# Projections by seven block products, three edits to attention, rows and last sums, in a 256-token layer stack of fp32

## Chip, cores and metric

The kernel runs on one core of a Trainium2 chip. The metric is the device time of one execution in microseconds; the kernel before has a median of 1836.27 us over 3 runs. TensorE multiplies matrices; VectorE (DVE), ScalarE (ACT) and GpSimd (POOL) do the element-wise work; SyncE (SP) issues the loads of weights. Each engine runs its own program, in order, and they meet at semaphores.

## What is computed

256 tokens of width 1024 in fp32 pass one hybrid layer (two kinds of attention, then a mixture of 16384 single-neuron experts) and then a second block of two layers (mixer, cross attention, convolutional feed-forward), which the change does not touch. The hybrid layer, cut:

```python
def hybrid_layer(x, cos, sin, norm1_g, w_in, ..., w_out, norm2_g, peer_wq, peer_k1, peer_k2, peer_u, peer_v):
    h = rmsnorm(x, norm1_g)
    (aq, ak, av, bq, bkc, bvc, bks, bvs, bkw, bvw, bgate, mgate) = split_columns(h @ w_in)
    ...
    ya = moba_attention(qa, ka, heads(av, A_HEADS)).reshape(B, S, A_WIDTH)
    ...
    yb = nsa_attention(qb, kc, vc, ks, heads(bvs, B_KV_HEADS), kw, heads(bvw, B_KV_HEADS), gb)
    ...
    merged = g[:, :, 0] * (ya @ w_up_a) + g[:, :, 1] * (yb @ w_up_b)
    x = x + merged @ w_out
    return x + peer_ffn(rmsnorm(x, norm2_g), peer_wq, peer_k1, peer_k2, peer_u, peer_v)

def peer_ffn(h, w_q, sub_k1, sub_k2, expert_u, expert_v):
    ...
    def per_chunk(args):
        xc, ec, gc = args
        u = expert_u[ec]
        a = jnp.einsum('cd,chkd->chk', xc, u).astype(jnp.float32)
        w = (jax.nn.gelu(a) * gc).astype(xc.dtype)
        return jnp.einsum('chk,chkd->cd', w, expert_v[ec])
```

In the experts each token has 8 heads; a head takes the best 16 of 128 by each half key and then the best 16 of their 256 pairs. The first 2560 of the columns of `h @ w_in` (queries, keys, values of both attentions) are the projections that the change rewrites.

## The kernel before

**Weights.** They come as slots of 1 MB into a ring of 4 slots, issued by SP in the fixed order of the program: key and value weights of the cross attention, projections (`proj`, 10 slots, two for each 512 columns), compression, gates, merge, output, routing queries, and 128 + 128 slots of experts. A slot is loaded again once TensorE is through with the one four places earlier (`slot_done`).

**Projections.** VectorE normalises x (`rms_rows`, L1490 to 1509) and TensorE turns it to `xT`. Meanwhile TensorE does memory keys (`feature_major`, L442). Then, for each of five chunks `c` of 512 columns, TensorE does two token tiles x eight k tiles of 512 columns (L556 to 565, matmul L451); ScalarE copies the two PSUM banks to `qkv` (L1171). VectorE clears and casts some tiles (L1512 to 1517), normalises and rotates the heads in four groups (`head_norm`, L1520 to 1569), makes the shifted and position-added copies (L1578 to 1587). TensorE goes on with gates (L569, L442) and turns the heads (L590).

**Attention.** 16 units, first eight of the one kind ("moba"), then eight of the other ("nsa"), in a pipeline of hand-written order. In step u TensorE does the scores of unit u (L617 to 637), the filling work (L682 to 714), then `turn_probs(u - 1)` (L640 to 654) and `values(u - 2)` (L656 to 678). VectorE takes maxima (L1602) and scales (L1626 to 1638), ScalarE takes exponentials and copies the turned probabilities (L1213 to 1225). The scores of unit u wait for `probT_ready` of unit u - 1.

**Experts.** 152 tokens are computed densely: each block of 128 experts is a matmul against all of them (`up_block` L827, `down_block` L835), with the gates from VectorE. The other 104 "sparse" tokens get the rows of their chosen experts by indirect DMA from GpSimd (L2271), 107 of `u_rows` and 107 of `v_rows`, each for up to 128 token-expert pairs, into seven buffers (`ROWS`). VectorE takes a dot product with each u row (`row_dots`, L1749) and later adds each v row, weighted (`row_adds`, L1850). Routing on VectorE is, for the second token tile, a loop over eight heads (L1794 to 1802: best 16, candidates, `pick` L1765 to 1786 after each four), then the loop over tiles (L1805 to 1835), in which the row numbers and gates are staged for GpSimd (L1820 to 1828). Dots go in numbers fixed by constants: up to `DOTS_ROUTING` between routing steps, up to `DOTS_FIRST` before the selection `sel` that TensorE needs for its first expert block (L1859); the rest is mixed among the gate work of the blocks. `LAST_ADDS` row sums stand at the end between the residual of the first token tile (L1916) and the fold of the sparse tokens (TensorE, L954); the second block starts on the first token tile at L922.

## Time and profile before

| quantity | value |
|---|---|
| median of 3 runs | 1836.27 us (1835.15 to 1836.65) |
| profiled execution | 1835.7 us, of which 1833.9 us are the span of the trace |
| mean granted clock of TensorE | 0.984 of full speed |
| busy share of TensorE, its weight loads | 96%, 81% |
| busy share of VectorE, ScalarE, GpSimd | 56%, 14%, 16% |
| DMA | 439.57 MB, mean 240 GB/s |

The trace has one row per instruction or group of like ones, with start, length and, where the engine stood idle before, what it waited for. The views used are the page's busy shares, the list of waits of an engine (what it waited for, in sum), the chain that ended last, groups of instructions of one line and shape, the timeline of an engine, and windows (busy time of each engine in a stretch with granted clock and share of the DMA). Along the span the DMA is above 0.9 of its capacity at 415 GB/s from about 440 to 1040 us, and at a third to a half elsewhere.

### The profile page before, as it was taken

How to read it: one execution, taken by the hardware profiler on the slowest of the kernel's cores; microseconds unless marked ns; L12 is line 12 of the kernel's file. 1: busy time of each engine (PE TensorE's matmuls, PEld its weight loads, DVE VectorE, ACT ScalarE, POOL GpSimd, SP SyncE). 2: the span in 40 equal slices, each digit the busy share in tenths (PEclk: the TensorE clock that was granted, in tenths of full speed). 3: DMA queues.
4: the chain of work that ended last, by engine and by line, in shares of the span. 5: the costliest groups of instructions: out<-in, count | busy, mean ns of one | idle time of the engine just before them, and what ended most of it. 6: DMA issues, size and time to landing. Idle time of an engine off the chain costs nothing.

```text
span 1833.9 us, 28803 instructions
## 1 busy us (share of the span) xinstructions
PE 1767.6 (96%) x11513; PEld 1477.1 (81%) x11513; DVE 1032.5 (56%) x2254; ACT 254.9 (14%) x603; POOL 295.1 (16%) x280
## 2 busy tenths in 40 slices
PE   8999989999999999999999689999999999999996
PEld 6478647886999999999999566789965977699942
DVE  1421342386964988899443653259984213269964
ACT  1013540120444111000000010111100001111100
POOL 0200000003333454344332510000000000000000
PEclk9999999999999999999999789999999999999998
DMA  7435232437999999999999963274454434354551
GB/s 277 162 124 175 72 113 92 166 117 286 418 416 416 414 416 411 369 415 414 416 416 418 368 259 115 92 252 162 165 180 159 162 138 148 128 184 161 171 174 46
DMA packets 76397, 439.57 MB, mean 240 GB/s; under 512 B 8530, under 2 KB 8560, under 8 KB 37504
## 3 DMA queue, kind: packets, MB, share of 16 engines
q1 hardware_dynamic: 42336, 304.11, 44.2%
q0 software_dynamic: 32528, 126.44, 17.5%
q10 hardware_dynamic: 1424, 7.47, 1.0%
q8 instruction: 80, 1.31, 0.3%
q14 instruction: 29, 0.24, 0.0%
HBM read 432.67 MB, written 5.24 MB: 239 GB/s over the span
## 4 chain that ended last, share of the span: by engine, by line
PE 70%; DMA 13%; DVE 9%; issue 6%; ACT 1%; POOL 0%; DVEq 0%; POOLq 0%
PE ps L1067 12%; PE ps L484 10%; PE ps L526 8%; PE ps L827 7%; PE ps L835 7%; PE ps L442 6%; DMA arena<-v_rows,sparse_pairs 6%; DMA arena<-u_rows,sparse_pairs 6%; PE ps L1088 4%; PE ps L451 4%; DVE arena L1850 2%; DVE arena L1749 2%; PE ps L695 2%; PE ps L742 2%; PE ps L848 1%
## 5 line engine op out<-in xcount | busy, mean ns | idle before, releaser
L827 PE MATMUL ps<-xT,ring 128*128 128x152 f32 x2048 | 271.6, 294 | 3.5 <-DVE sel L1859 3.4
L827 PEld LDWEIGHTS ps<-xT,ring 128*128 128x128 f32 x2048 | 267.2, 191 | 4.4 <-DVE sel L1859 3.7
L835 PE MATMUL ps<-arena,ring 128*128 128x152 f32 (+1 forms) x2048 | 269.6, 293 | 0.1
L835 PEld LDWEIGHTS ps<-arena,ring 128*128 128x128 f32 x2048 | 265.5, 190 | 0.8 <-issue 0.8
L484 PE MATMUL ps<-ring,arena 128*128 128x512 f32 x416 | 181.4, 592 | 0.4 <-ACT arena L1371 0.4
L1850 DVE SCALAR_TENSOR_TENSOR arena<-arena,sparse_dots 128x1024 f32<-128x1024 f32 x105 | 134.7, 1283 | 76.1 <-DMA arena<-v_rows,sparse_pairs 68.4
L526 PEld LDWEIGHTS ps<-xT,ring 128*128 128x128 f32 x1536 | 173.4, 192 | 3.0 <-issue 2.9
L526 PE MATMUL ps<-xT,ring 128*128 128x128 f32 x1536 | 174.1, 275 | 0.0
L1749 DVE CUSTOM_DVE_ANT_0 arena<-arena 128x1024 f32<-128x1024 f32 x107 | 128.2, 1223 | 78.6 <-DMA arena<-u_rows,sparse_pairs 71.3
L2271 POOL DMA_INDIRECT arena<-u_rows,sparse_pairs x107 | 129.7, 1213 | 188.9 <-DVE sparse_dots L1749 153.5
L2271 POOL DMA_INDIRECT arena<-v_rows,sparse_pairs x107 | 130.2, 1216 | 179.8 <-DVE arena L1850 121.6
L2236 POOL TENSOR_SCALAR stat<-stat 128x1 f32<-128x1 f32 (+2 forms) x23 | 4.4, 190 | 942.5 <-DVE stat L2014 711.9
L484 PEld LDWEIGHTS ps<-ring,arena 128*128 128x128 f32 x416 | 78.0, 190 | 93.0 <-issue 92.1
L442 PE MATMUL ps<-xT,ring 128*128 128x256 f32 x544 | 121.4, 386 | 0.0
L442 PEld LDWEIGHTS ps<-xT,ring 128*128 128x128 f32 x544 | 105.1, 194 | 14.6
L1067 PE MATMUL ps<-arena 128*128 128x128 f32 x864 | 102.4, 275 | 0.0
L1067 PEld LDWEIGHTS ps<-arena 128*128 128x128 f32 x864 | 99.4, 192 | 0.0
L1067 PE MATMUL ps<-xT,ring 128*128 128x128 f32 x576 | 70.2, 275 | 0.0
L1602 DVE CUSTOM_DVE_ANT_0 arena<-ps,small 128x128 f32<-128x128 f32 (+1 forms) x48 | 14.6, 355 | 97.0 <-PE ps L630 65.6
L451 PE MATMUL ps<-ring,xT 128*128 128x512 f32 x160 | 68.8, 592 | 0.0
L1067 PEld LDWEIGHTS ps<-xT,ring 128*128 128x128 f32 x576 | 67.2, 192 | 0.0
L451 PEld LDWEIGHTS ps<-ring,xT 128*128 128x128 f32 x160 | 30.4, 190 | 37.8 <-issue 37.8
(305 smaller groups left out, 2108.0 us busy)
## 6 DMA issues: line engine op xcount, KB each, us to landing
ring<-stream SPq DMA_DIRECT2D x288, 1024.0 KB
arena<-second_params POOLq DMA_DIRECT2D x6, 1024.0 KB, 5.2
arena<-kv_scratch POOLq DMA_DIRECT2D x2, 2048.0 KB, 13.3
kv_scratch<-arena POOLq DMA_DIRECT2D x2, 1024.0 KB, 6.7
kv_scratch<-arena ACTq DMA_DIRECT2D x2, 1024.0 KB
arena<-held_params ACTq DMA_DIRECT2D x1, 2048.0 KB
arena<-u_rows,sparse_pairs POOLq DMA_INDIRECT x107
arena<-v_rows,sparse_pairs POOLq DMA_INDIRECT x107
```

What stands on the lines that cost most here:

```text
L442: ins = pe.matmul(ps[:, bank, t * T:(t + 1) * T], w[:, k * 2 * P + t * P:k * 2 * P + (t + 1) * P], act[:, k, :], start=(k == 0), stop=(k = ...
L451: ins = pe.matmul(ps[:, bank0 + i, :], act[:, k0 + k, i * P:(i + 1) * P], w[:, k * 512:(k + 1) * 512], start=(first_k and k == 0), stop=(l ...
L484: ins = pe.matmul(ps[:, bank0 + 2 * i + hf, :], act_of(2 * s + k, i), held[s][:, k * D + hf * 512:k * D + (hf + 1) * 512], start=(bank0 + ...
L526: ins = pe.matmul(ps[:, bank, t * T + i * P:t * T + (i + 1) * P], held[s][:, k * 2 * P + t * P:k * 2 * P + (t + 1) * P], xT[:, k, i * P:(i ...
L695: ins = pe.matmul(ps[:, 6, t * T:(t + 1) * T], w[:, k * 2 * P + t * P:k * 2 * P + (t + 1) * P], xT[:, k, :], start=(k == 0), stop=(k == KT ...
L827: ins = pe.matmul(ps[:, o % 2, 0:DENSE], w[:, (o % 2) * D + k * P:(o % 2) * D + (k + 1) * P], xT[:, k, 0:DENSE], start=(k == 0), stop=(k = ...
L835: ins = pe.matmul(ps[:, 4 + k // 2, c:c + DENSE], w[:, (o % 2) * D + k * P:(o % 2) * D + (k + 1) * P], H[:, n, :], start=False, stop=last, ...
L1067: ins = pe.matmul(ps[:, bank + b, c * P:(c + 1) * P], weight[:, k, :], x[:, k, :], start=(k == 0), stop=(k == 3))
L1088: return pe.matmul(ps[:, bank, :], x, weight, start=(m == 0), stop=(m == FT_PAIRS - 1 and bank < 4))
L1749: dve.tensor_tensor_reduce(fetched[:, b, :], fetched[:, b, :], x_sparse[:, m // PAIRS_HALF, :], 1.0, 0.0, ALU.mult, ALU.add, dots[:, 0, m: ...
L1850: dve.scalar_tensor_tensor(total, fetched[:, b, :], dots[:, 0, m:m + 1], total, ALU.mult, ALU.add).then_inc(row_added, 1)
L2271: pool.indirect_dma_start(fetched[:, b, :], None, table, bass.IndirectOffsetOnAxis(ap=pairs[:, 0, m:m + 1].bitcast(U32), axis=0), bounds_c ...
```

## The change

**Projections.** Each chunk of 512 columns is made as a 2 x 2 by 2 x 2 block product (token tiles x halves of k, halves of k x halves of columns) with seven block products in place of eight. VectorE makes four sums of weight blocks (`sums_of_proj`) for each chunk and four sums of blocks of `xT` once, and puts the seven products together (`add_proj`); ScalarE copies the first product only. The order on VectorE is written out anew: the clears and casts and the second to fourth head norms stand behind output sums. `qkv_copied` gives way to five semaphores.
**Attention.** `values(u - 2)` stands ahead of `turn_probs(u - 1)`; the scores wait for `probc_copied` of unit u - 2, and only where that unit is "nsa", instead of `probT_ready` of unit u - 1; ScalarE copies that tile first.
**Rows.** The row numbers are staged in halves, after heads 4 and 8 of the loop over heads, with two row dots behind each of heads 5 to 8; the gates are sent later. GpSimd fetches 15 rows from the first half before it waits for the second. `DOTS_ROUTING` is 38, `DOTS_FIRST` 56.
**Last sums.** `LAST_ADDS` is 16.

The diff, cut:

```diff
@@ -46,9 +46,12 @@
 CHUNKS = PAIRS_HALF + PAIRS_B
-DOTS_ROUTING = 30
-DOTS_FIRST = 50
-LAST_ADDS = 21
+PH_LATE = 4
+DOTS_HEAD = 2
+DOTS_EARLY = DOTS_HEAD * PH_LATE
+DOTS_ROUTING = 38
+DOTS_FIRST = 56
+LAST_ADDS = 16
@@ -220,13 +223,22 @@
...
         memT = mem_raw.rearrange("p (k t) -> p k t", k=KT)
+        p_sums = [prob_and_PT[:, 0:4096].rearrange("p (s k n) -> p s k n", s=4, k=4),
+                  gT.rearrange("p j t -> p (j t)").rearrange("p (s k n) -> p s k n", s=4, k=4)]
+        px_sums = yT.rearrange("p j t -> p (j t)").rearrange("p (s k n) -> p s k n", s=4, k=4)
+        p_first = xn[:, 0, 0:512].rearrange("p (b n) -> p b n", b=2)
+        p_sum2 = xn[:, 0, 512:768]
+        p_sum43 = xn[:, 1, 0:512].rearrange("p (s n) -> p s n", s=2)
...
@@ -555,14 +569,36 @@
             for c in range(5):
...
+                b0, sums = 4 * (1 - c % 2), p_sums[c % 2]
...
+                def product(b, half, x, weight):
+                    for k in range(4):
+                        ins = pe.matmul(ps[:, b0 + b, half * T:(half + 1) * T], x[:, k, :], weight[:, k, :],
+                                        start=(k == 0), stop=(k == 3))
+                    return ins
+                if c < 2:
+                    pe.wait_ge(xkv_ready, 1)
                 else:
...
-                for kh in range(2):
-                    w = slot("proj", 2 * c + kh)
-                    token_major(w, 4 + 2 * (c % 2), xT, 4 * kh, 4, kh == 0, kh == 1)\
-                        .then_inc(slot_done, 1)
+                    pe.wait_ge(proj_added, c - 1)
+                w1 = slot("proj", 2 * c).rearrange("p (k n) -> p k n", k=4)
+                product(0, 0, x11, w1[:, :, 0:T])
+                w2 = slot("proj", 2 * c + 1).rearrange("p (k n) -> p k n", k=4)
+                product(0, 1, x12, w2[:, :, 0:T]).then_inc(proj_psum, 1)
+                if c == 0:
+                    pe.wait_ge(xkv_ready, 3)
+                    pe.wait_ge(proj_x_ready, 1)
+                product(2, 0, x4, w2[:, :, T:2 * T])
+                pe.wait_ge(proj_w_ready, c + 1)
+                product(1, 0, x1, sums[:, 0]).then_inc(slot_done, 1)
+                product(1, 1, x3, sums[:, 2]).then_inc(slot_done, 1)
+                if c == 0:
+                    pe.wait_ge(xkv_ready, 4)
+                product(3, 0, x2, sums[:, 1])
+                product(2, 1, x22, sums[:, 3]).then_inc(proj_psum, 1)
+            pe.wait_ge(proj_added, 4)
@@ -579,7 +615,7 @@
-            pe.wait_ge(qkv_copied, 10)
+            pe.wait_ge(proj_added, 5)
@@ -622,7 +658,8 @@
                     pe.wait_ge(max_ready, u if kind == "nsa" else u - 1)
-                    pe.wait_ge(probT_ready, u - 1)
+                    if units[u - 2][0] == "nsa":
+                        pe.wait_ge(probc_copied, u - 1 - NU // 2)
@@ -725,10 +762,10 @@
                     fill(u)
+                if u >= 2:
+                    values(u - 2)
                     turn_probs(u - 1)
-                if u >= 2:
-                    values(u - 2)
@@ -1166,10 +1203,8 @@
             for c in range(5):
-                act.wait_ge(slot_done, START["proj"] + 2 * c + 2)
-                for i in range(TT):
-                    act.copy(qkv[:, i, c * 512:(c + 1) * 512], ps[:, 4 + 2 * (c % 2) + i, :])\
-                        .then_inc(qkv_copied, 1)
+                act.wait_ge(proj_psum, 2 * c + 1)
+                act.copy(p_first[:, c % 2, :], ps[:, 4 * (1 - c % 2), 0:T]).then_inc(proj_first, 1)
@@ -1217,11 +1252,11 @@
                 pt = PT[:, u % 2].rearrange("p k n -> p (k n)")
+                if kind == "nsa":
+                    act.copy(pt[:, 8 * P:9 * P], ps[:, 2 * (u % 2), 0:P]).then_inc(probc_copied, 1)
                     ins = act.copy(pt[:, a * P:a * P + w], ps[:, 4 + a // 4, 0:w])
-                if kind == "nsa":
-                    ins = act.copy(pt[:, 8 * P:9 * P], ps[:, 2 * (u % 2), 0:P])
...
@@ -1484,6 +1519,34 @@
+            def sums_of_proj(c):
+                w1, w2, w3, w4 = (p_sums[c % 2][:, n] for n in range(4))
+                wb = []
+                for n in (START["proj"] + 2 * c, START["proj"] + 2 * c + 1):
+                    dve.wait_ge(loaded[n % RING], 16 * (n // RING + 1))
+                    w = ring[:, n % RING, :].rearrange("p (k n) -> p k n", k=4)
+                    wb += [w[:, :, 0:T], w[:, :, T:2 * T]]
+                w11, w12, w21, w22 = wb
+                link(dve.tensor_tensor(w1, w12, w11, ALU.subtract))
+                dve.tensor_tensor(w3, w22, w12, ALU.subtract)
+                link(dve.tensor_tensor(w2, w22, w1, ALU.subtract))
+                dve.tensor_tensor(w4, w21, w2, ALU.subtract).then_inc(proj_w_ready, 1)
+            def add_proj(c):
+                b0, col = 4 * (1 - c % 2), 512 * c
+                dve.wait_ge(proj_first, c + 1)
+                dve.wait_ge(proj_psum, 2 * c + 2)
+                link(dve.tensor_tensor(p_sum2, p_first[:, c % 2, :], ps[:, b0 + 3, 0:T], ALU.add))
+                dve.tensor_tensor(qkv[:, 0, col:col + T], p_first[:, c % 2, :], ps[:, b0, T:2 * T], ALU.add)
+                link(dve.tensor_tensor(p_sum43, p_sum2.unsqueeze(1).to_broadcast([P, 2, T]),
+                                       ps[:, b0 + 1, :].rearrange("p (s n) -> p s n", s=2), ALU.add))
+                dve.tensor_tensor(qkv[:, 0, col + T:col + 2 * T], p_sum43[:, 0, :], ps[:, b0 + 2, 0:T], ALU.add)
+                dve.tensor_tensor(qkv[:, 1, col:col + T], p_sum43[:, 1, :], ps[:, b0 + 2, T:2 * T], ALU.add)
+                dve.tensor_tensor(qkv[:, 1, col + T:col + 2 * T], p_sum43[:, 1, :], ps[:, b0 + 1, 0:T], ALU.add)\
+                    .then_inc(proj_added, 1)
...
@@ -1509,20 +1573,22 @@
             rms_rows(0)
...
+            dve.wait_ge(xT_by_dve, 4)
...
+            link(dve.tensor_tensor(x2, x1, x11, ALU.subtract))
+            dve.tensor_tensor(x3, x11, x21, ALU.subtract)
+            dve.tensor_tensor(x4, x12, x2, ALU.subtract).then_inc(proj_x_ready, 1)
+            sums_of_proj(1)
                 chunk = c0 // 512
-                dve.wait_ge(qkv_copied, 2 * chunk + 2)
+                dve.wait_ge(proj_added, chunk + 1)
@@ -1568,8 +1634,24 @@
-            for grp in range(4):
-                head_norm(grp)
+            add_proj(0)
+            sums_of_proj(2)
+            head_norm(0)
+            add_proj(1)
+            sums_of_proj(3)
...
+            add_proj(2)
+            sums_of_proj(4)
+            add_proj(3)
+            add_proj(4)
+            head_norm(1)
+            head_norm(2)
+            head_norm(3)
@@ -1789,6 +1871,19 @@
+            def stage_rows(half):
...
+                first, second = (routed[rows, 1, n, half * PAIRS_HALF:(half + 1) * PAIRS_HALF]
+                                 .rearrange("p (m r) -> p r m", r=2) for n in range(2))
+                for r, dst in enumerate((pairs, pairs_out)):
+                    ins = dve.scalar_tensor_tensor(dst[rows, 0, c].bitcast(U32), first[:, r], float(P), second[:, r],
+                                                   ALU.mult, ALU.add)
+                ins.then_inc(pairs_staged, 1)
+                if half == 0:
+                    dve.wait_ge(x_sparse_ready, 1)
@@ -1798,10 +1893,12 @@
                     shift_gates()
+                if h >= PH - PH_LATE:
+                    row_dots(DOTS_HEAD)
                     pick(1, h - 3, 4)
-            dve.wait_ge(x_sparse_ready, 1)
+                    stage_rows(h // 4)
@@ -1818,14 +1915,12 @@
                     up_rows, b_rows = slice(P - SPARSE_A, P), slice(0, P // 2)
-                    for dst, rows, h0, n in ((pairs, up_rows, 0, PAIRS_HALF),
-                                             (pairs_out, up_rows, PAIRS_HALF, PAIRS_HALF),
-                                             (pairs_out_b, b_rows, 0, P)):
-                        dve.scalar_tensor_tensor(dst[rows, 0, 0:n].bitcast(U32), routed[rows, 1, 0, h0:h0 + n],
...
-                        dve.tensor_copy(dst[rows, 1, 0:n], gf[rows, h0:h0 + n])\
-                            .then_inc(pairs_staged, 1)
+                    gates_of = gf[up_rows].rearrange("p (m r) -> p r m", r=2)
+                    for r, dst in enumerate((pairs, pairs_out)):
+                        dve.tensor_copy(dst[up_rows, 1, 0:PAIRS_HALF], gates_of[:, r])
+                    dve.scalar_tensor_tensor(pairs_out_b[b_rows, 0, 0:P].bitcast(U32), routed[b_rows, 1, 0, :],
...
+                    dve.tensor_copy(pairs_out_b[b_rows, 1, 0:P], gf[b_rows]).then_inc(pairs_staged, 1)
...
@@ -2262,8 +2357,13 @@
-            pool.wait_ge(pairs_staged, 3)
-            pool.dma_start(pairs[0:SPARSE_A, :, 0:PAIRS_HALF], pairs_out[SPARSE_A:P]).then_inc(pairs_in, 16)
+            def rows_of(half):
+                c = slice(half * PAIRS_HALF // 2, (half + 1) * PAIRS_HALF // 2)
+                pool.wait_ge(pairs_staged, half + 1)
+                pool.dma_start(pairs[0:SPARSE_A, 0, c], pairs_out[SPARSE_A:P, 0, c]).then_inc(pairs_in, 16)
+            rows_of(0)
@@ -2285,9 +2385,14 @@
                 if m == PAIRS_HALF:
-                    pool.wait_ge(pairs_in, 16 * (1 + SETS_B))
+                    pool.wait_ge(pairs_in, 16 * (3 + SETS_B))
                 fetch_u(m)
-                if m == 3:
+                if m == ROWS + DOTS_EARLY - 1:
+                    rows_of(1)
+                    pool.wait_ge(pairs_in, 32)
+                if m == ROWS + DOTS_EARLY + 1:
+                    pool.wait_ge(pairs_staged, 3)
+                    pool.dma_start(pairs[0:SPARSE_A, 1, 0:PAIRS_HALF], pairs_out[SPARSE_A:P, 1]).then_inc(pairs_in, 16)
```

## Rows read from the trace of the kernel before

**Rows 1.** The page's busy shares: busy us, share of the span, instructions.
```profile
PE 1767.6 (96%) x11513; PEld 1477.1 (81%) x11513; DVE 1032.5 (56%) x2254; ACT 254.9 (14%) x603; POOL 295.1 (16%) x280
```

**Rows 2.** Waits of TensorE, whole run: us in total, times, longest.
```profile
PE ps L922 <- DVE xT L1916: 17.5, 1, 17.5
...
PE ps L649 <- DVE arena L1638: 6.0, 8, 2.5
PE ps L954 <- DVE arena L1850: 5.9, 1, 5.9
PE ps L827 <- DVE sel L1859: 3.4, 1, 3.4
PE ps L630 <- ACT arena L1222: 3.2, 6, 1.1
PE ps L633 <- ACT arena L1224: 2.5, 4, 0.6
```

**Rows 3.** Chain that ended last, 30 to 150 us: start, length, link.
```profile
31.62 6.91 PE ps L442 x32
38.53 68.67 PE ps L451 x160
```

**Rows 4.** VectorE groups by shape, 38 to 107 us: busy, mean ns, idle.
```profile
L1529 DVE TENSOR_TENSOR arena<-arena 128x1024 f32<-128x1024 f32 x3 | 3.7, 1225 | 22.7 <-ACT arena L1171 22.7
...
L1548 DVE TENSOR_TENSOR arena<-arena,small 128x256 f32<-128x256 f32 x2 | 0.8, 422 | 0.0
```

**Rows 5.** The same view, 1233 to 1345 us, in the feed-forward.
```profile
L2094 DVE TENSOR_TENSOR arena<-ring,arena 128x512 f32<-128x512 f32 x17 | 11.8, 692 | 0.6
```

**Rows 6.** Timeline of VectorE, 53 to 127 us: start, length, [idle before].
```profile
53.47 1.22 DVE L1529 TENSOR_TENSOR arena<-arena 128x1024 f32<-128x1024 f32 x1 [15.60 <-ACT arena L1171]
...
63.15 0.49 DVE L1568 TENSOR_TENSOR arena<-arena 128x128 f32<-128x128 f32 x2
...
125.77 1.15 DVE L1587 TENSOR_TENSOR arena<-arena,small 128x120 f32<-128x120 f32 x4
```

**Rows 7.** Timeline of TensorE at 148 us, the turning of the heads.
```profile
148.49 3.26 PE L590 MATMUL ps<-small,arena 128*128 128x128 f32 x28
```

**Rows 8.** Timeline of TensorE, 246 to 262 us, in attention.
```profile
252.54 1.58 PE L677 MATMUL ps<-arena 128*64 128x128 f32 x16
...
260.32 0.66 PE L677 MATMUL ps<-arena 128*64 128x128 f32 x8
...
261.60 0.70 PE L633 MATMUL ps<-arena 64*128 64x512 f32 x2 [0.61 <-ACT arena L1224]
```

**Rows 9.** Timeline of GpSimd, the first row fetch.
```profile
430.62 1.15 POOL L2271 DMA_INDIRECT arena<-u_rows,sparse_pairs  x1 [2.88 <-DMA sparse_pairs<-arena]
```

**Rows 10.** Timeline of VectorE, 390 to 594 us: first pick, dots.
```profile
390.48 0.27 DVE L1785 TENSOR_TENSOR arena<-arena 128x64 f32<-128x64 f16 x1
...
441.16 1.23 DVE L1749 CUSTOM_DVE_ANT_0 arena<-arena 128x1024 f32<-128x1024 f32 x1 [10.20 <-DMA arena<-u_rows,sparse_pairs]
...
593.25 1.22 DVE L1749 CUSTOM_DVE_ANT_0 arena<-arena 128x1024 f32<-128x1024 f32 x1 [1.91 <-DMA arena<-u_rows,sparse_pairs]
```

**Rows 11.** Windows: length, busy PE, PEld, DVE, ACT, POOL, clock, DMA share, GB/s.
```profile
391.00:400.00 9.00, 9.00 (x49) 8.08 (x48) 8.45 (x42) 1.51 (x3) 0.00 (x0) 1.00 0.34 119
595.30:599.00 3.70, 3.70 (x21) 3.67 (x22) 3.67 (x4) 0.00 (x0) 0.97 (x1) 0.61 1.03 422
745.00:750.00 5.00, 5.00 (x53) 4.99 (x51) 4.97 (x6) 0.00 (x0) 2.91 (x2) 1.00 0.48 133
1066.00:1069.00 3.00, 3.00 (x15) 3.00 (x15) 0.42 (x1) 0.00 (x0) 0.00 (x0) 0.50 0.02 5
```

**Rows 12.** Timeline of VectorE, the last row sums in one group.
```profile
1036.77 29.06 DVE L1850 SCALAR_TENSOR_TENSOR arena<-arena,sparse_dots 128x1024 f32<-128x1024 f32 x21
```

**Rows 13.** Timeline of TensorE, 1030 to 1082 us: first tile, fold.
```profile
1036.01 10.20 PE L922 MATMUL ps<-xT,ring 128*128 128x128 f32 x64 [17.54 <-DVE xT L1916]
...
1065.88 7.05 PE L954 MATMUL ps<-small,arena 128*128 128x64 f32 x32 [5.94 <-DVE arena L1850]
```

More of the change, by code:

```diff
@@ L222, in build @@
         kcT = a1.take(P)
+        mark_prob = a1.at
         prob = a1.take(2 * 1024).rearrange("p (b k n) -> p b k n", b=2, k=4)
@@ L336, in build @@
         x_ready = sem("x_ready")
-        qkv_copied = sem("qkv_copied")
+        proj_x_ready, proj_w_ready = sem("proj_x_ready"), sem("proj_w_ready")
+        proj_psum, proj_first, proj_added = sem("proj_psum"), sem("proj_first"), sem("proj_added")
         bgate_psum, gb_ready = sem("bgate_psum"), sem("gb_ready")
@@ L557, in _ @@
             for c in range(5):
-                if c >= 2:
-                    pe.wait_ge(qkv_copied, 2 * (c - 1))
-                else:
-                    pe.wait_ge(xkv_ready, 2 * c + 2)
-                for kh in range(2):
-                    w = slot("proj", 2 * c + kh)
-                    token_major(w, 4 + 2 * (c % 2), xT, 4 * kh, 4, kh == 0, kh == 1)\
-                        .then_inc(slot_done, 1)
+                b0, sums = 4 * (1 - c % 2), p_sums[c % 2]
+                x11, x12, x22 = xT[:, 0:4, 0:P], xT[:, 4:8, 0:P], xT[:, 4:8, P:T]
+                x1, x2, x3, x4 = (px_sums[:, n] for n in range(4))
+                def product(b, half, x, weight):
[5 more added lines that the diff above has]
+                    pe.wait_ge(xkv_ready, 1)
+                else:
+                    pe.wait_ge(proj_added, c - 1)
[15 more added lines that the diff above has]
+            pe.wait_ge(proj_added, 4)
             pe.wait_ge(first_in, 16)
@@ L1498, in rms_rows @@
                         scaled(i)
+                    sums_of_proj(0)
                     dve.wait_ge(small_in, 16)
@@ L1511, in _ @@
             rms_rows(0)
-            dve.tensor_copy(iota_ah[:], sm("iota")[:, 0:TOPK].unsqueeze(2).to_broadcast([P, TOPK, PH]))
-            dve.tensor_copy(iota16[:], sm("iota")).then_inc(iota_ready, 1)
-            dve.memset(zeros[:], 0.0).then_inc(zeros_ready, 1)
-            dve.memset(flat.rearrange("p k j n -> p (k j n)"), 0.0)
-            dve.memset(kc2, 0.0)
-            link(dve.memset(vc2, 0.0))
+            dve.wait_ge(xT_by_dve, 4)
+            x11, x12 = xT[:, 0:4, 0:P], xT[:, 4:8, 0:P]
+            x21, x22 = xT[:, 0:4, P:T], xT[:, 4:8, P:T]
+            x1, x2, x3, x4 = (px_sums[:, n] for n in range(4))
+            link(dve.tensor_tensor(x1, x21, x22, ALU.add))
+            link(dve.tensor_tensor(x2, x1, x11, ALU.subtract))
+            dve.tensor_tensor(x3, x11, x21, ALU.subtract)
+            dve.tensor_tensor(x4, x12, x2, ALU.subtract).then_inc(proj_x_ready, 1)
+            sums_of_proj(1)
             def head_norm(grp):
@@ L1790, in shift_gates @@
                     .then_inc(gate_shift, 1)
+            def stage_rows(half):
+                link(dve.memset(mark_cell[:], 0.0))
+                rows, c = slice(P - SPARSE_A, P), slice(half * PAIRS_HALF // 2, (half + 1) * PAIRS_HALF // 2)
+                first, second = (routed[rows, 1, n, half * PAIRS_HALF:(half + 1) * PAIRS_HALF]
[6 more added lines that the diff above has]
+                    dve.wait_ge(x_sparse_ready, 1)
             dve.memset(pairs_out_b[0:P // 2, :, P:], 0.0)
```

15 lines of the change are left out of this document (11 added, 4 removed).

## Prediction

> **What bounds the kernel now.** I read the page's busy shares first: TensorE is busy 1767.6 us of a 1833.9 us span [rows 1], so a gain must be TensorE work taken away or a wait of TensorE taken away. The list of what TensorE waits for comes next [rows 2]; it is short. Three stretches matter. In the projections there is no wait at all: the chain of the end runs through 160 matmul records of 512 columns in 68.67 us [rows 3], so only less work helps. In attention (166 to 277 us) the waits on VectorE's scaling and ScalarE's copies come to 6.0 + 3.2 + 2.5 = 11.7 us [rows 2]. Around the experts TensorE waits 3.4 us for VectorE's routing and rows, then 17.5 and 5.9 us for the rows' sums at the end [rows 2]. After 1102 us nothing is touched by the change, and I expect it only to move.
>
> **Part 1, projections by seven products.** Before, a chunk of 512 output columns is 16 matmuls of 512 columns. After, it is 7 products of 4 matmuls of 256 columns, 28 in place of 32 half-width ones. A matmul is two records here. A 256-column record takes 6.91 / 32 = 0.216 us, a 512-column one 68.67 / 160 = 0.429 [rows 3]; so 5 chunks x 28 x 2 x 0.216 = 60.5 us, against 68.7: **8.2 us less** if TensorE never waits. ScalarE gets less to do (one 256-column copy a chunk instead of two of 512).
>
> The cost is VectorE's. Weight sums: 4 instructions of 1024 elements a chunk at 1.225 us [rows 4] = 4.9 us. Output sums: five of 256 at 0.42 [rows 4] and one of 512 at 0.69 [rows 5] = 2.8 us. Activation sums, once: 4 x 0.69 = 2.8 us. So VectorE has 7.7 us a chunk under a TensorE chunk of 12.1 us. Laid out in order: the first weight sums need the second slot of the chunk, whose place in the ring comes free with the second key slot at about 22.8 us; I put its landing at 28, so the sums end near 33, the gains on xT near 35.5, the activation sums near 38.4. TensorE comes at 38.5 and needs them 5 us into the chunk. Chunks then end at 50.6, 62.7, 74.8, 86.9 and 99.0. VectorE: sums(1) to 49, add(0) to 53.4, sums(2) to 58.4, the first head norm (10.2 us, from 53.47 to 63.64 in the trace [rows 6]) to 68.6, add(1) to 71.4, sums(3) to 76.3, the moved clears and casts (5.2 us) to 81.5, add(2) to 84.3, sums(4) to 89.2, add(3) to 92.0, add(4) to 102. The needs of TensorE are 74.8, 80.0, 86.9 and 92.1 for add(1), sums(3), add(2) and sums(4): margins of 3.4, 3.7, 2.6 and 2.9 us. They hold, but by little.
>
> The second to fourth head norms now start at 102 and take 10.2 + 10.2 + 6.4, to 129; the shifted and position-added copies behind them (5.9 us, done at 126.9 now [rows 6]) go on to 135. TensorE has the gates between: it turns heads at 148.49 now [rows 7], at 140.3 then, and needs the copies at 143.4. Margin 8 us; nothing lost. ScalarE and GpSimd (the inverse roots) are queued behind nothing new.
>
> **Part 2, attention.** The values of unit u-2 are put ahead of the transposes of unit u-1. The transposes wait for VectorE's scaling; the values take 0.66 or 1.58 us [rows 8] and now run in that wait, 6.0 us over eight times with 2.5 for the longest [rows 2]: those go. In exchange nothing lies any more between the transposes and the next scores. In the first eight units these scores no longer wait for ScalarE's copy, so that 3.2 us goes as well. From unit 10 on they wait for one small copy that now goes first; before, with values between, the wait was 0 or 0.61 us [rows 8]. I take 0.5 us, six times = 3.0 us (bounds 0.3 and 0.8, as semaphore and copy have no row in this order). The last two units have less to cover them: the 2.5 us wait for the last scaling goes, since VectorE is no more held by values done late, and about 1.5 us of new waiting on ScalarE comes. 11.7 - 3.0 - 1.5 = **7.2 us less**; bounds 4 and 9.
>
> **Part 3, rows earlier.** The first row fetch is issued at 430.62 [rows 9], behind all eight heads. With half the rows' numbers ready at 390.75 (end of the first pick [rows 10]) plus some 4 us for staging and the small transfer, it is issued at about 395, into a DMA system that is a third busy (0.34 [rows 11]). Fifteen rows are fetched by 440; eight of their dots go between heads 5 to 8 (8 x 1.2 us, plus some 3 us for the first to land), which puts VectorE some 12 us behind; but it then sat idle 10.2 us for its first row at 441.16 [rows 10], and that wait is gone. So the routing of the second tile keeps its time within 2 us. GpSimd waits for the second half with 15 rows issued; seven of them are a full buffer, so nothing starves.
>
> What it gives: from 441.16 to 593.25 VectorE takes dots 2 to 50 at the DMA's pace, 3.17 us a row, and TensorE waits 3.4 us for the selection behind dot 50 [rows 2, 10]. With 15 landed at 447, dot 56 can be done at 447 + 41 x 3.17 = 577, before the 592 at which TensorE asks. The wait goes, and the slow clock behind it: 3.70 us at a granted 0.61 [rows 11] cost 3.7 x 0.39 = 1.4. **4.8 us less**, bounds 0 and 5.5.
>
> **The lead does not reach the end.** The program fixes that VectorE has done 96 dots when the first expert half ends and 48 sums when the second ends, before and after alike. And at 745 to 750 us the DMA is only 0.48 busy [rows 11]: the ring and all seven row buffers are full there already. An earlier start can't fill them more. So the stretch from 750 us on, in which the DMA is full again, brings the same bytes at the same time, and the 1.39 us a sum of the last 27 sums stays (29.06 us for the last 21 [rows 12]).
>
> **Part 4, 16 last sums for 21.** The first token tile is now released five sums (7.0 us) later, so TensorE's 17.54 us wait [rows 13] becomes 24.5. Its work under the last sums is 23.9 us (1036.01 to 1059.9), the 16 sums take 22.2: it comes to the fold at 1066.9 where it now starts at 1065.88 [rows 13]. That is +1.0 us. But the second wait, 5.94 us, is gone, and behind it the clock was at 0.50 [rows 11] through the 7.05 us of the fold [rows 13]; at full clock that is 3.5 us, and the next matmuls, too, start warm (some 1.7 us). Between -4.2 and +1.0 I take **3.0 us less**. The Trainium skill ("TensorE: Matmul & The Clock Gate", section "What's actually happening") says that an idle array falls to the lower of two clocks and that steady activity lifts it; by that rule one long wait costs the slow start once where two waits cost it twice, and the sum would be at the -4.2 end. The trace agrees so far as it shows both slow starts.
>
> Another rule speaks against the change. The rows are fetched from GpSimd's queue, and the issue of one takes 1.15 us in the trace [rows 9]. The Trainium skill ("SBUF — State Buffer", section "SBUF: two separate sides") says that GpSimd can't write its descriptors while VectorE holds the port they share; by it each early fetch would be up to one VectorE instruction (1.2 us) later, which lies inside the 15 us of slack at dot 56.
>
> **Sum**: 8.2 + 7.2 + 4.8 + 3.0 = 23.2 us. The profiled execution took 1835.7 us (span 1833.9), the median of the runs is 1836.27, 0.6 above: 1836.27 - 23.2 = **1813.0 us**.
>
> **Rivals.**
> (B) The rows' lead is carried to the end. Then both waits there (23.4 us) and their slow clock (some 5 us) go, in place of my 3.0: 1813.0 - 25.4 = 1787.6. Against it is the half idle DMA at 745 us [rows 11]. 5%.
> (C) VectorE runs late in the projections: each margin is under 4 us. If its work is a third dearer than the nearest rows, TensorE waits 1 to 2 us a chunk and 4 to 8 us of the 8.2 are lost: 1817 to 1821. 17%.
> (D) The waits in attention or at the selection only change their place: the selection now stands behind six more dots (6 x 3.17 = 19 us of rows); if only the seven buffered rows come early (7 x 3.17 = 22 us) most of the slack is gone. 3 to 8 us lost: 1816 to 1821. 14%.
> (E) Slower. Every added VectorE instruction costs twice its nearest row. A chunk is then 15.4 us against 12.1, the fourth and fifth wait for their sums, and TensorE turns heads some 15.5 us later than before; with the other parts' 15 that is no gain, and each such wait of over 3 us brings a clock fall of 1.4 to 5 us: 1841 to 1852. It decides from about twice the price on. Against it, the same kind of sums read from the ring in the feed-forward take 0.692 us for 512 elements [rows 5], no more than others. 4%.
>
> **How the numbers follow.** Forecast 60%; B 5, C 17, D 14, E 4. The forecast's own range is 1808 to 1817 by the bounds of its terms; with C and D the range is 1805 to 1822. A measurement of this kernel tells about 0.2% (3.7 us) from no change. Faster takes all but E and a corner of C and D together: 0.94; within 0.2%: 0.03; slower: 0.03.
>
> **What would show it.** Step 1: 280 records of 0.216 us at the new product line without idle time before them, ending near 99 us; any wait there on VectorE's sums is C. Step 2: TensorE's waits between 160 and 270 us sum to some 5 us, none on VectorE's scaling. Step 3: first fetch near 395 us before the shift, no wait for the selection, a DMA even idler just after the first expert half. Step 4: one wait of some 24 us before the first token tile, none before the fold, and full clock in the fold. If TensorE's last wait for rows is much under 20 us, the reasoning on the lead was wrong.

## The result, and the profile after

The changed kernel takes 1808.67 us (median of 4 runs, 1808.12 to 1809.24) against 1836.46 (1835.15 to 1836.75) for the kernel before, a ratio of 0.9849 with a 95% interval of 0.9834 to 0.9864: 27.8 us less, forecast 23.2 less. The profiled execution took 1809.13 us, with a span of 1807.3 for 1833.9; the spans differ by 26.6 us, and the other 1.2 are the distances of the two profiled executions from their medians (1835.7 against 1836.46, 1809.13 against 1808.67).

The page's busy shares after:

```profile
PE 1750.7 (97%) x11633; PEld 1491.7 (83%) x11633; DVE 1071.6 (59%) x2312; ACT 252.3 (14%) x598; POOL 292.4 (16%) x282
```

TensorE's work fell by 16.9 us against [rows 1] and VectorE's rose by 39.1. The waits of TensorE, which answer to [rows 2]:

```profile
PE ps L959 <- DVE xT L2011: 23.9, 1, 23.9
...
PE ps L670 <- ACT arena L1256: 3.0, 6, 0.7
PE ps L709 <- ACT arena L1259: 2.2, 2, 1.3
PE ps L885 <- DVE e L1973: 1.6, 1, 1.6
PE ps L872 <- DMA ring<-stream: 0.4, 1, 0.4
```

Gone are the wait for VectorE's scaling (6.0), for the selection (3.4) and before the fold (5.9). New is a wait of 1.6 us for the first one-hots, and the wait before the first token tile (L959, before L922) is longer.

TensorE passes the same places in both traces, so the whole span can be cut into stretches with nothing left over:

| stretch of TensorE | before, us | after, us | difference | forecast |
|---|---|---|---|---|
| before the projections | 38.36 | 37.95 | -0.4 | 0 |
| projections | 68.67 | 60.44 | -8.2 | -8.2 |
| 24-column matmuls and next weights, to the turning of the heads | 41.46 | 39.79 | -1.7 | 0 |
| heads and attention | 128.57 | 121.51 | -7.1 | -7.2 |
| merge to the first expert block | 181.03 | 181.02 | 0 | 0 |
| first experts to the first gates | 140.78 | 137.19 | -3.6 | -4.8 |
| first gates to the last expert block | 419.60 | 419.89 | +0.3 | 0 |
| from there to the second block's output product | 83.50 | 78.64 | -4.9 | -3.0 |
| second block | 713.61 | 713.60 | 0 | 0 |
| behind TensorE's last matmul | 18.3 | 17.3 | -1.0 | 0 |

The sum is -26.6 us, the difference of the two spans. VectorE's last sums lie 25.5 us earlier in the trace, as TensorE's last matmul does; so what differs in the last line lies behind them, where nothing in the change touches the program.

### The profile page after: what moved, and what is told of

Its sections match the earlier page's. It is cut to its first block, busy times and chain, and to the rows that moved or that the text cites. A ratio compares the mean times of both kernels' runs of the same rounds, so it can differ in the third digit from the quotient of the medians.

```text
span 1807.3 us, 29102 instructions
## 1 busy us (share of the span) xinstructions
PE 1750.7 (97%) x11633; PEld 1491.7 (83%) x11633; DVE 1071.6 (59%) x2312; ACT 252.3 (14%) x598; POOL 292.4 (16%) x282
## 4 chain that ended last, share of the span: by engine, by line
PE 86%; DMA 8%; DVE 3%; issue 1%; ACT 1%; POOL 0%; DVEq 0%; POOLq 0%; ACTq 0%
PE ps L864 15%; PE ps L1104 12%; PE ps L498 10%; PE ps L540 9%; PE ps L456 9%; PE ps L872 6%; DMA arena<-v_rows,sparse_pairs 6%; PE ps L1125 4%; PE ps L578 3%; DMA arena<-u_rows,sparse_pairs 2%; PE ps L732 2%; PE ps L779 2%; PE ps L842 2%; PE ps L745 1%; DVE arena L1945 1%; PE ps L959 1%
## 5 line engine op out<-in xcount | busy, mean ns | idle before, releaser
L2371 POOL DMA_INDIRECT arena<-u_rows,sparse_pairs x107 | 126.0, 1177 | 213.4 <-DVE sparse_dots L1831 183.6
L456 PE MATMUL ps<-xT,ring 128*128 128x256 f32 x544 | 120.2, 383 | 0.0
L456 PEld LDWEIGHTS ps<-xT,ring 128*128 128x128 f32 x544 | 104.1, 192 | 14.2
L1351 ACT ACTIVATE arena<-ps 128x152 f32 x128 | 38.1, 298 | 141.5 <-PE ps L864 141.2
L1125 PE MATMUL ps<-arena 128*128 128x512 f32 x112 | 52.8, 594 | 0.3
## 6 DMA issues: line engine op xcount, KB each, us to landing
arena<-u_rows,sparse_pairs POOLq DMA_INDIRECT x107, 13.1
```

The source lines that it names most:

```text
L456: ins = pe.matmul(ps[:, bank, t * T:(t + 1) * T], w[:, k * 2 * P + t * P:k * 2 * P + (t + 1) * P], act[:, k, :], start=(k == 0), stop=(k = ...
L1125: return pe.matmul(ps[:, bank, :], x, weight, start=(m == 0), stop=(m == FT_PAIRS - 1 and bank < 4))
L1351: act.activation(H[:, n, :], ps[:, b, 0:DENSE], ACT.Gelu_apprx_tanh).then_inc(expert_gelu, 1)
L2371: pool.indirect_dma_start(fetched[:, b, :], None, table, bass.IndirectOffsetOnAxis(ap=pairs[:, 0, m:m + 1].bitcast(U32), axis=0), bounds_c ...
```

## Experiments

Each kernel is the changed one with one edit, unless it says otherwise. Medians are of 4 runs; the ratio is to the kernel before, run on the same chip. The kernel before took 1835.95 to 1838.42 us in the median from set to set, so a difference of one or two us between medians of different sets is not shown to be an edit's.

**Old projections** (`old_proj`): the five chunks, ScalarE's copies and VectorE's order are those of before.

```diff
+                for kh in range(2):
+                    w = slot("proj", 2 * c + kh)
+                    token_major(w, 4 + 2 * (c % 2), xT, 4 * kh, 4, kh == 0, kh == 1)\
+                        .then_inc(slot_done, 1)
...
+            for grp in range(4):
+                head_norm(grp)
```

> The changed kernel with the projections of before (sixteen 512-column matmuls a chunk, ScalarE copies, old order on VectorE); the three other parts stay. Theory (my accounting of the two traces): the products give 8.2 us of work, and about 2 us more come from the slow clock behind the projections being shorter (the granted clock was 0.50 for some 7 us there before, 0.50 to 0.8 for some 4 us after); all of it comes back, so 1808.7 + 10.3 = 1819.0 us. Rival 1: only the 8.2 us of work hang on this part, the clock does not: 1816.9. Rival 2: an earlier start is partly eaten up by the rows and loads later: under 1815.

Measured: 1817.77 us (1814.46 to 1818.59), ratio 0.9895 (0.9878 to 0.9913); 9.1 us of the 10.3 come back. The timeline of TensorE says which:

```profile
38.88 68.83 PE L464 MATMUL ps<-ring,xT 128*128 128x512 f32 x160
107.54 3.65 PE L582 MATMUL ps<-arena,xT 128*128 128x24 f32 x32
111.03 36.47 PE L455 MATMUL ps<-xT,ring 128*128 128x256 f32 x160
```

The 68.7 us are back (107.54 less 38.88), but the 24-column matmuls and the weights behind them take 3.65 and 36.47 us, to the hundredth as in the changed kernel (3.65 at L605 and 36.47 at L456), not 4.07 (L569) and 37.73 (L442) as in the kernel before. So the 1.7 us of the table's third line don't hang on the products. The median lies between the theory (1819.0) and rival 1 (1816.9) and the runs spread over both; the timeline decides for rival 1. 8.2 us are this part's, and in the trace another 0.9 is a start that was later here. The start moves by itself: in the twelve traces with the changed kernel's projections it lies between 37.95 and 39.47 us.

**Attention, all of it undone** (`old_attn`) and **in half** (`turn_first`: only the order on TensorE).

```diff
-                if u >= 2:
-                    values(u - 2)
                 if 1 <= u <= NU:
                     turn_probs(u - 1)
+                if u >= 2:
+                    values(u - 2)
```

> The changed kernel with the attention order of before. Theory: TensorE gained 7.1 us between the turning of the heads and the merge, so 1808.7 + 7.1 = 1815.8 us, with TensorE's waits for VectorE's scaling back at about 6 us and for ScalarE's copies about 6 us. Rival: part of the 7.1 us came from VectorE's and ScalarE's queues being emptier after the new projections, so less comes back: 1812 to 1814.

> The changed kernel with the transposes of unit u-1 ahead of the values of unit u-2 again, as before the change; the new, rarer wait of the scores and ScalarE's order stay. It splits the 7.1 us of attention. Theory (the order hides the scaling, the new wait only ScalarE's copy): TensorE waits for VectorE's scaling some 5.9 us again, its waits for ScalarE are under 2 us (with values between the two, the small copy is done), total 1808.7 + 5.9 - 3.5 = 1811 us. Rival (the order gave all of it, the waits for ScalarE stay at 5 us as in the changed kernel): 1814.6. Rival (the new wait gave nearly all): under 1810.

Measured: `old_attn` 1816.28 us (1815.86 to 1818.13), `turn_first` 1810.81 us (1809.49 to 1811.6). So all the edits together give 7.6, the order on TensorE alone 2.1, the rarer wait with ScalarE's order 5.5; the last two were not taken apart. Both theories hold (1815.8 and 1811). The waits of TensorE between 140 and 290 us, first `old_attn`:

```profile
PE ps L685 <- DVE arena L1719: 5.9, 8, 2.4
PE ps L666 <- ACT arena L1256: 3.2, 6, 1.1
PE ps L669 <- ACT arena L1258: 2.4, 4, 0.6
PE ps L669 <- ACT arena L1256: 0.9, 2, 0.5
PE ps L708 <- DVE arena L1726: 0.5, 1, 0.5
...
```

Then `turn_first`:

```profile
PE ps L686 <- DVE arena L1720: 6.0, 8, 2.4
PE ps L709 <- DVE arena L1727: 0.5, 1, 0.5
PE ps L779 <- DVE arena L1727: 0.4, 1, 0.4
PE ps L732 <- ACT arena L1215: 0.3, 1, 0.3
```

With the new semaphore the scores wait for ScalarE no more (L732, a 0.3 us wait of the filling work, is in the changed kernel too) while the values still lie between the transposes and the next scores. Putting the values first then takes away 6.0 us of waits for VectorE and brings 5.2 us of waits for ScalarE (3.0 and 2.2 in the changed kernel), since nothing covers the small copy any more. The order moves a wait more than it removes one: in waits it is worth 1.3 us (6.5 for 5.2). What is above that is the clock. From the turning of the heads to the merge `turn_first` takes 124.46 us, 2.95 more than the changed kernel's 121.51, and in it the granted clock is 0.50 from 256 to 262 us, behind the longest wait:

```profile
254.89 1.42 PE L686 MATMUL ps<-small,arena 128*128 128x128 f32 x8 [2.45 <-DVE arena L1720]
```

`old_attn` has the same fall and takes 131.00 us; the kernel before, with the same waits in the same order and the same 2.45 us wait, keeps the clock at 1.00 there and takes 128.57.

**Rows as late as before** (`old_rows`):

```diff
-DOTS_ROUTING = 38
-DOTS_FIRST = 56
+DOTS_ROUTING = 30
+DOTS_FIRST = 50
...
-                if h >= PH - PH_LATE:
-                    row_dots(DOTS_HEAD)
```

> The changed kernel with the rows' start of before (all row numbers after the eighth head, 30 and 50 dots), and 16 last sums as in the changed kernel. Theory (the lead never reaches the end): the 3.4 us wait for the selection and 1.6 us of slow clock come back, the new 1.6 us wait for the first gates goes, and the end is 0.6 us later: 1808.7 + 4.0 = 1812.7 us; TensorE's wait before the first token tile stays at 24 to 25 us; and the DMA is full again from 620 to 740 us, where the changed kernel has it at 380 to 390 GB/s. Rival (the lead is carried to the end): that wait grows by the whole lead, 15 us or more, to over 1823 us.

Measured: 1815.4 us (1814.96 to 1815.64), 6.7 slower than the changed kernel. The waits of TensorE and three windows of it, with the same windows of the changed kernel behind:

```profile
PE ps L959 <- DVE xT L1998: 23.4, 1, 23.4
...
PE ps L864 <- DVE sel L1941: 5.9, 1, 5.9
```

```profile
620.00:640.00 20.00, 20.00 (x192) 19.91 (x191) 18.35 (x27) 2.68 (x9) 9.59 (x7) 1.00 1.02 407
680.00:700.00 20.00, 20.00 (x192) 19.91 (x192) 18.66 (x28) 2.67 (x9) 10.00 (x7) 1.00 1.02 413
720.00:740.00 20.00, 20.00 (x162) 18.02 (x161) 13.73 (x15) 1.04 (x4) 5.49 (x4) 1.00 0.81 303
```

```profile
620.00:640.00 20.00, 20.00 (x192) 19.91 (x192) 15.51 (x21) 2.68 (x9) 7.06 (x6) 1.00 1.00 393
680.00:700.00 20.00, 20.00 (x192) 19.91 (x191) 15.55 (x23) 2.68 (x9) 5.98 (x6) 1.00 1.00 390
720.00:740.00 20.00, 20.00 (x179) 18.71 (x179) 19.46 (x20) 0.00 (x0) 8.39 (x6) 1.00 0.80 285
```

The wait at the end is 23.4 us without the early rows and 23.9 with them, and the DMA is fuller without them: the lead is spent between 620 and 740 us in a DMA that waits for buffers (from 600 to 745 us GpSimd, which issues the fetches, waits 62.5 us for VectorE's dots in the changed kernel and 48.4 here). That part of the theory holds. The size was off (1815.4 us for 1812.7): the wait for the selection is 5.9 us, not 3.4, and the stretch from the first experts to the first gates is 6.4 us longer (143.61 for 137.19). The 50 dots took some 2.6 us longer from the first fetch than in the kernel before (166.4 for 163.8 us); why, no run shows.

**21 last sums** (`last21`: `LAST_ADDS = 21`).

> The changed kernel with 21 last sums for 16. Theory (two slow starts against one): the wait before the first token tile is 17.0 us (five sums of 1.38 us less), a second wait of 5.9 us stands before the fold, and the fold and the matmuls behind it run at the slow clock again: 1808.7 + 4.5 = 1813.2 us. Rival (the sums set the time whichever way they are divided, the clock gives nothing): 1808.7 + 0 to 1.0.

Measured: 1813.57 us (1812.73 to 1814.1). The timeline of TensorE:

```profile
1014.34 10.03 PE L959 MATMUL ps<-xT,ring 128*128 128x128 f32 x64 [17.07 <-DVE xT L2011]
...
1044.20 7.05 PE L991 MATMUL ps<-small,arena 128*128 128x64 f32 x32 [6.09 <-DVE arena L1945]
1051.05 8.81 PE L959 MATMUL ps<-xT,ring 128*128 128x128 f32 x64
```

The changed kernel, the same places:

```profile
1021.65 10.06 PE L959 MATMUL ps<-xT,ring 128*128 128x128 f32 x64 [23.86 <-DVE xT L2011]
...
1045.29 3.66 PE L991 MATMUL ps<-small,arena 128*128 128x64 f32 x32
1048.78 7.39 PE L959 MATMUL ps<-xT,ring 128*128 128x128 f32 x64
```

The waiting is nearly the same (23.2 against 23.9 us in sum). What differs is the clock behind the second wait: 3.4 us of fold and 1.4 us of the next matmuls. The granted clock is 0.50 from 1046 to 1049 us in the one and 1.00 from 1045 to 1048 in the other. The medians differ by 4.9 us; in the traces the way from the first gates to the second block's output product is 3.9 us longer (502.5 for 498.5).

**More dots in the first half** (`u104`). GpSimd's waits go by a row's place in the order, so that any number holds; else only this:

```diff
-U_FIRST = 96
+U_FIRST = 104
```

> The changed kernel with 104 dots, not 96, in the first expert half (the rows' order moves with it; the dots among the gates go from 40 to 48). It asks why the rows' lead is lost. Theory (the counts fixed by the program keep the lead from passing on: at 620 to 740 us the DMA moves 380 to 390 GB/s and at 720 to 740 us 285, for 416 elsewhere, because all row buffers are full): the DMA moves 416 GB/s through 620 to 720 us, eight rows of 0.52 MB (about 10 us of the full DMA) are ahead at the end, the wait before the first token tile falls from 23.9 to about 14 us, total 1799 us. Rival (VectorE is full in this stretch: 2.5 dots of 1.3 us and 3.8 us of gates are 7.1 us a group, for 7.4 us of TensorE's): the gates come late, TensorE waits in the first half, and the total is 1805 to 1812.

Measured: 1797.16 us (1796.66 to 1797.37), ratio 0.9779 (0.9761 to 0.9796): 11.5 us faster than the changed kernel. Its wait of TensorE and two windows:

```profile
PE ps L959 <- DVE xT L2011: 13.1, 1, 13.1
```

```profile
680.00:700.00 20.00, 20.00 (x191) 19.94 (x188) 17.70 (x26) 2.68 (x9) 8.78 (x7) 1.00 1.02 415
720.00:740.00 20.00, 20.00 (x185) 19.19 (x185) 19.42 (x21) 0.00 (x0) 9.49 (x7) 1.00 0.95 361
```

390 GB/s have become 415 and the wait is 10.8 us shorter, as eight rows more were ahead. The fixed count, not the DMA, kept these rows from the end. No run has 104 dots with the late start of the rows, so how much of the 11.5 us needs the early start is open.

**First one-hots early** (`gates_early`):

```diff
+                if hf == 0:
+                    one_hots(0, 0, 0, 0, first=True)
                 dve.wait_ge(expert_gelu, HALF_BLOCKS * (hf + 1))
```

> The changed kernel with the first group of one-hots made before VectorE waits for the 64th block's activation (they don't need it). It asks whether the new 1.6 us wait of TensorE for the first gates is the order of these two. Theory: yes; the selection ends at 571.8 us, the one-hots then end at 575.0 and TensorE asks at 576.3: wait gone, 1808.7 - 1.6 = 1807.1 us. Rival: the wait is the selection's, the one-hots would be late anyway: 1808.7.

Measured: 1806.33 us (1804.83 to 1807.52). The 1.6 us wait is gone from the list, so it was the order of these two; the wait before the first token tile is 24.5 us in place of 23.9. The 2.3 us between the medians are under the 2.7 us that these four runs spread over, so the gain in time is not shown.

**24-column matmuls interleaved** (`spread24`): one of them behind each of the 32 matmuls of the next weights (`bc`).

> The changed kernel with the 32 matmuls of 24 columns interleaved one by one with the 256-column matmuls of the next weights, not all in a row. It asks what the slow clock behind the projections is from (granted 0.50 for about 4 us behind them here, about 7 us in the kernel before). Theory (the stretch of 24-column matmuls is what lets the clock fall): the clock stays at 1.00, and 1.5 to 2 us go: 1807. Rival (the clock falls whatever the order of these, or falls longer, as 64 matmuls now are thinly fed): 1808.7 to 1811.

Measured: 1807.35 us (1806.23 to 1808.49). Windows of this kernel, then of the changed one:

```profile
103.00:105.00 2.00, 2.00 (x15) 1.85 (x13) 0.83 (x1) 0.00 (x0) 1.00 (x2) 1.00 0.03 8
```

```profile
103.00:105.00 2.00, 2.00 (x6) 1.63 (x5) 0.64 (x1) 0.00 (x0) 1.19 (x2) 0.50 0.00 0
```

The clock doesn't fall in this trace, and TensorE turns the heads at 136.68 us for 138.18. But the other traces don't let the interleaving have the credit. First the changed kernel, then `u104`, which has the same program up to here, with the 24-column matmuls in a row:

```profile
98.39 3.65 PE L605 MATMUL ps<-arena,xT 128*128 128x24 f32 x32
101.88 36.47 PE L456 MATMUL ps<-xT,ring 128*128 128x256 f32 x160
```

```profile
99.21 3.65 PE L605 MATMUL ps<-arena,xT 128*128 128x24 f32 x32
102.70 34.78 PE L456 MATMUL ps<-xT,ring 128*128 128x256 f32 x160
103.00:105.00 2.00, 2.00 (x11) 1.77 (x10) 1.43 (x2) 0.11 (x1) 0.36 (x2) 1.00 0.00 0
```

The granted clock stays at 1.00 there in `u104`, and so it does in `turn_first`, `old_rows`, `last21` and `sums_twice`; it falls in the kernel before, the changed kernel, `old_proj`, `old_attn` and `gates_early`. From the start of the projections to the turning of the heads `spread24` takes 98.54 us and `u104` 98.54. So the interleaving is worth at most the fall, some 1.7 us. The four interleaved traces (this and the three of the last group) have none and five of the ten others have one; that fits the theory and doesn't show it.

**Weight sums made twice** (`sums_twice`, chunks 1 to 4).

> The changed kernel with VectorE's four weight sums of chunks 1 to 4 made twice (4.9 us more a chunk, nothing else changed). It asks how thin the cover over VectorE's work is. Theory (order and durations of the trace): the second sums still hold; output sums of chunk 1 end 5.2 us late, weight sums of chunk 3 another 4.6 us, output sums of chunk 2 1.0 us, weight sums of chunk 4 4.6 us: 15.4 us of TensorE's waits in four places and 1 to 5 us of slow clock behind them: 1825 to 1829 us. Rival (a thick cover: the later head norms and casts take it up): under 1818.

Measured: 1823.52 us (1822.42 to 1824.27), 14.9 slower. Waits of TensorE, and two groups of the timeline behind them:

```profile
PE ps L578 <- DVE arena L1539: 5.8, 2, 3.3
PE ps L578 <- DVE arena L1552: 4.7, 1, 4.7
```

```profile
80.39 5.41 PE L578 MATMUL ps<-ring,xT 128*128 128x256 f32 x16 [4.65 <-DVE arena L1552]
...
107.39 7.13 PE L578 MATMUL ps<-arena 128*128 128x256 f32 x24 [3.26 <-DVE arena L1539]
```

10.5 us of waits, not 15.4 (a TensorE that is late once needs the next sums later), and three slow starts of 1.8 us each (5.41 and 7.13 for 3.62 and 5.34). So 4.9 us more a chunk are more than VectorE's cover holds, as margins of 2.6 to 3.7 us in the forecast say.

**Putting it together.** `best1` has the edits of `gates_early` and `spread24`, with `U_FIRST = 107` and `LAST_ADDS = 17`. `best2` adds `DOTS_HEAD = 5`, `DOTS_ROUTING = 50`, `DOTS_FIRST = 64` and six row sums in the first half, for which ScalarE takes the activation of the first 64 dots between the halves. `best3` is `best2` with `DOTS_HEAD = 4`, `DOTS_ROUTING = 46` and `LAST_ADDS = 15`.

> Three edits of the runs before together (first one-hots early, 24-column matmuls interleaved), all 107 dots in the first half in place of 104, and 17 last sums for 16. Theory (the end is set by when the last row is summed, so only what brings rows forward or cuts work behind them counts): against the run with 104 dots three rows more are ahead (3.8 us), one more last sum releases the first tile 1.4 us earlier and costs nothing at the fold (23.6 us of sums under 24.0 us of TensorE work), the interleaving gives 1.3, the early one-hots next to nothing at the end, since the rows' time there does not move with TensorE: 1797.2 - 6.5 = 1790.7 us. Rival (each saving counts in full): 1788 to 1789. Rival (VectorE is full in the first half: 2.7 dots a group are 7.3 us for TensorE's 7.4): waits on the gates and over 1797.

> The same, with five dots for two behind each of heads 5 to 8, 64 dots ahead of the selection, and six row sums already in the first half (ScalarE takes the activation of the first 64 dots between the halves). It asks whether the lead is as large as the number of rows that are used up by then, and nothing else. Theory: six more rows are used by the end of the first half (107 + 6 for 107), the DMA has room for them at 380 to 440 us, where the changed kernel moves 263 to 373 GB/s of 416; the end comes 6 x 1.26 = 7.6 us earlier than in the run with 107: 1790.7 - 7.6 = 1783 us, if dot 64 is done when TensorE asks for the selection. Rival (it is not, and VectorE has no room for 15 us more among the heads): a wait for the selection of 3 us or more with a slow clock, and 1788 or more.

> The last kernel with four dots for five behind each of heads 5 to 8, and 15 last sums for 17. In its trace VectorE came late with the gates of both tiles, ScalarE stood in line for them with TensorE's copies behind it (waits of TensorE of 2.5 and 3.9 us, and a slow clock), and 17 sums lay under 21.4 us of TensorE's work at the end (a wait of 3.2 us, a slow fold and slow start). Theory (all three come from these two numbers): one dot less a head is 3.9 us at the first gates and 5.2 us at the second, more than either wait; two sums less are 2.8 us: 1796.6 - 6.4 - 3 - 3.2 - 3.4 = 1780.6 us. Rival (the rows now are late, as four less are ahead by 440 us): the wait before the first tile is 5 us or more and the total 1785 or more.

Measured: 1797.98 us (1796.58 to 1798.86), 1796.56 (1793.67 to 1797.6) and 1790.67 (1787.99 to 1796.93; ratio 0.9754, 0.9728 to 0.978). All three miss what I expected. `best1`, timeline of TensorE, then `best2` and `best3`, waits:

```profile
1001.88 7.38 PE L963 MATMUL ps<-xT,ring 128*128 128x128 f32 x64 [2.77 <-DVE xT L2018]
...
1029.21 7.04 PE L995 MATMUL ps<-small,arena 128*128 128x64 f32 x32 [6.21 <-DVE arena L1949]
```

```profile
PE ps L869 <- ACT arena L1356: 3.9, 1, 3.9
PE ps L996 <- DVE arena L1953: 3.2, 1, 3.2
...
PE ps L847 <- ACT arena L1336: 2.5, 1, 2.5
```

```profile
PE ps L869 <- DVE sel L1962: 8.4, 1, 8.4
...
PE ps L964 <- DVE xT L2024: 0.6, 1, 0.6
PE ps L996 <- DVE arena L1953: 0.4, 1, 0.4
```

In `best1` the rows did come three further (the last sum ends at 1029 us, in `u104` at 1032.6), but the second wait and its slow clock were back. Behind a first wait of only 2.8 us the clock stayed full and the first tile took 7.4 us, not the changed kernel's 10.1, so TensorE had 21.1 us of work over the last sums, not 23.6; and there were 17 sums, of which one waited 2.5 us for its row. TensorE also waited 3.2 us for one-hots in the first half. In `best2` VectorE was late with the gates, ScalarE stood waiting for them in its queue, and TensorE's copies were queued behind that. In `best3` dot 64 ended at 580.4 us, for 566.7 with five dots a head, and the selection was 8.4 us late. `best3` has the lowest median here, but its four runs spread over 9 us and their slowest is in the range of `best2` and `u104`. Its two waits at the end are down from 23.4 us [rows 2] to 1.0.

## Why the forecast came out as it did

**Projections.** Held as written: 60.44 us measured for 60.5, with no wait. The margins held too. Output sums of chunk 1 and 2 end at 71.2 and 83.6 us on VectorE, where TensorE needs them at 74.2 and 86.3: 3.0 and 2.7 us, forecast 3.4 and 2.6. `sums_twice` shows how near rival (C) was: with the weight sums made twice TensorE waits. Where between the two the loss begins, no run shows. What the forecast did not have is the slow clock behind the 24-column matmuls, 6.8 us long before and 3.4 us after; `old_proj` has 3.4 us too and five traces of the same matmuls have none, so the 1.7 us can't be credited to the change.

**Attention.** Held, 7.1 us for 7.2, and the split held too. The forecast let VectorE's 6.0 us go for 4.5 us of new waits for ScalarE, a net of 1.5 for the order, which leaves 5.7 of its sum for the new wait and ScalarE's order. New waits of 5.2 us came (3.0 us in six, as forecast, and 2.2 for the last two, forecast 1.5); `turn_first` gives the order 1.3 us in waits and 2.1 in time, and the rest 5.5. What was missed is small: two more of the old waits went (0.9 and 0.5 us in `old_attn`), so 13.1 us of waits went, not 11.7. The step to distrust is the reading of 2.1 us: both traces with the old order have a slow clock that the kernel before does not have.

**Rows.** The mechanism held, and so did its place: the first fetch is issued at 376.7 us, forecast 395 less the 17.4 us shift, that is 378:

```profile
376.73 1.15 POOL L2371 DMA_INDIRECT arena<-u_rows,sparse_pairs  x1 [1.98 <-DMA sparse_pairs<-arena]
```

The selection's wait is gone. The term was 4.8 and came to 3.6, because a smaller wait took its place (rival (D) in small): the one-hots stood behind a wait for the 64th block that they don't need, 1.6 us, shown by `gates_early`. The wait and the slow clock of some 1.7 us behind it, 0.50 for 3.4 us in the trace before, are gone. The Trainium skill's rule on GpSimd's descriptors ("SBUF — State Buffer", section "SBUF: two separate sides"), cited ahead, cost nothing visible: the fetch instructions of the u rows took 1.18 us in the mean after, 1.21 before. The section ties the rule to VectorE's two-port modes; whether the dots and sums here run in one, no trace shows.

**The lead doesn't reach the end.** Held: the last wait is 23.9 us with it, 23.4 in `old_rows`. The reason was half of it. The forecast named ring and buffers at 745 us; the DMA fell behind from 620 us on, and `u104` puts its root in the fixed 96 dots. That rival (B) was turned down rightly hangs on this constant: with 104 dots 10.8 of the 23.9 us of the wait go.

**Last sums.** The mechanism held and the term was mis-sized, 3.0 for 4.9 us, the largest miss. The forecast had -4.2 as one end of its bounds and took less. The waits came out at 23.9 us for 23.5 before, 0.4 longer where it allowed 1.0, and the slow clock behind the second wait went whole (3.4 us of fold, 1.6 behind it). The Trainium skill's rule ("TensorE: Matmul & The Clock Gate", section "What's actually happening"), that an idle array falls to the lower clock and activity lifts it, would have given the -4.2; the trace agrees, and `last21` puts the price at 3.9 us between the traces and 4.9 between the medians. It should have decided the term.

Of the 26.6 us between the two spans, 3.1 (the start 0.4, the clock 1.7, the end 1.0) were in no term of the sum, and no run ties them to an edit; what is left is 23.5 for a forecast of 23.2. That it comes so near is in part luck: the rows gave 1.2 us less than their term and the last sums 1.9 more.

## What to carry to other kernels

Before crediting a reordering with the wait that it covers, ask what the moved work was covering until now, and test order and semaphore apart; they may trade one wait for another. A lead in a pipeline with fixed counts is worth only as many items as the counts let it use, so move the counts with the start. And where waits can't be avoided, one long wait can beat two short ones by a slow start of TensorE's clock, here 3.9 us in the traces for 23 to 24 us of waiting either way. Last, look for a stretch in every trace that has it before crediting an edit with it: half of the traces with the same 24-column matmuls had a slow clock behind them and half had none.

## What the runs showed of the hardware

TensorE's clock can fall without any idle time: behind 32 back-to-back matmuls of 24 columns the granted clock was 0.50 (1.2 GHz) for 6.8 us in the kernel before and for 3.4 us in four other traces, with TensorE busy throughout, and stayed at 1.00 (2.4 GHz) in five traces with the same matmuls in a row. It cost 1.7 us in the changed kernel (36.47 us for 34.78).

The same waits don't always bring the same clock: behind a wait of 2.45 us in attention the granted clock was 0.50 for 6.8 us in `old_attn` and `turn_first` and stayed at 1.00 in the kernel before. So one trace of a kernel doesn't tell whether such a fall is the kernel's or this execution's.
